# Two transformer blocks on one core: VectorE's small work around the convolution moved, and ScalarE's two norm visits put earlier

## The reference, cut to what matters

```python
proj = jnp.einsum('bld,dp->blp', n, w_in)
conv_in, gates, scal = jnp.split(proj, [CONV_CH, CONV_CH + GATE_CH], axis=-1)
c = jax.nn.silu(centred_dwconv(conv_in, conv_w, conv_b)).astype(F32)
q, k, v, xs, Bm, Cm = jnp.split(c, [...], axis=-1)
...
q = l2_normalize(q.reshape(Bsz, L, gh, GDN_HEAD_DIM)) * (GDN_HEAD_DIM ** -0.5)
k = l2_normalize(k.reshape(Bsz, L, gh, GDN_HEAD_DIM))
g_fw = -jnp.exp(gA[0]) * jax.nn.softplus(a_f + gB[0])
...
gc = jnp.cumsum(g, axis=-1)
decay = jnp.exp(jnp.where(incl, gc[..., :, None] - gc[..., None, :], -jnp.inf))
```

## Time and profile before

| | us |
|---|---|
| runs | 1373.17, 1374.37, 1367.18 |
| median | 1373.17 |
| the profiled execution: its time | 1375.73 |
| the profiled execution: its span | 1373.7 |
| TensorE busy | 1226.6 (89%) |
| VectorE busy | 645.5 (47%) |
| ScalarE busy | 410.6 (30%) |
| GpSimd busy | 331.0 (24%) |

### The profile page before, as it was taken

One profiled execution on the slowest core, in us unless ns is written; L12 is line 12 of the kernel. 1 busy time (PEld: TensorE's weight loads), 2 busy tenths in 40 slices (PEclk: granted clock), 3 DMA queues, 4 the chain that ended last, 5 costly groups with the idle time before them and its releaser, 6 DMA issues.

```text
span 1373.7 us, 17987 instructions
## 1 busy us (share of the span) xinstructions
PE 1226.6 (89%) x7446; PEld 926.1 (67%) x7446; DVE 645.5 (47%) x1059; ACT 410.6 (30%) x991; POOL 331.0 (24%) x322
## 2 busy tenths in 40 slices
PE   6989789899999699978789998998988999899887
PEld 5878655577754332212129797998878889798777
DVE  1597758133560300001026355575887245466785
ACT  4345542133631410100014521311524441230332
POOL 0386640412200300000021122132253112223231
PEclk9999989999999799999999999999999999999999
DMA  5333333766406699999982435153332245335310
GB/s 196 123 123 123 123 92 134 267 242 218 152 30 275 257 386 421 422 421 422 421 340 71 160 107 204 62 173 134 123 111 85 96 172 170 114 114 184 123 62 31
DMA packets 91554, 257.02 MB, mean 187 GB/s; under 512 B 7645, under 2 KB 12534, under 8 KB 79058
## 3 DMA queue, kind: packets, MB, share of 16 engines
q1 hardware_dynamic: 89122, 248.67, 48.3%
q0 software_dynamic: 2032, 6.95, 1.6%
q10 hardware_dynamic: 320, 0.26, 0.1%
HBM read 253.49 MB, written 2.12 MB: 186 GB/s over the span
## 4 chain that ended last, share of the span: by engine, by line
PE 63%; DMA 14%; DVE 9%; ACT 7%; POOL 5%; issue 2%; SPq 0%; DVEq 0%; ACTq 0%; POOLq 0%
PE bank L686 59%; DMA ring<-in_w_up_dram 8%; DMA ring<-in_w_down_dram 4%; PE bank L695 3%; DVE ring_r L1993 3%; POOL late L2595 3%; POOL acc L2596 2%; DVE acc L2064 2%; ACT ring L1508 1%; DMA ring<-in_w_ada_dram 1%; ACT cT L1508 1%; ACT L1508 1%; ACT oa L1508 1%; ACT qkT L1508 1%; ACT xT L1508 0%
## 5 line engine op out<-in xcount | busy, mean ns | idle before, releaser
L2698 POOL CAST w_hi_r<-ring 128x1024 fp32r<-128x1024 f32 x136 | 151.0, 1138 | 670.4 <-DMA ring<-in_w_in_dram 267.3
L686 PE MATMUL bank<-ring_r,xT_hi 128*128 128x256 f32 (+1 forms) x864 | 245.9, 285 | 0.0
L686 PE MATMUL bank<-w_hi_r,xT_hi 128*128 128x256 f32 x704 | 208.6, 296 | 24.2 <-DVE ring_r L1993 19.8
L686 PE MATMUL bank<-w_hi_r,xT_r 128*128 128x256 f32 x704 | 202.6, 288 | 0.0
L1993 DVE TENSOR_TENSOR ring_r<-ring,w_hi_r 128x1024 fp32r<-128x1024 f32 x136 | 182.6, 1375 | 41.9 <-POOL w_hi_r L2698 41.9
L686 PEld LDWEIGHTS bank<-ring_r,xT_hi 128*128 128x128 f32 x864 | 168.3, 195 | 0.2
L686 PEld LDWEIGHTS bank<-w_hi_r,xT_hi 128*128 128x128 f32 x704 | 137.2, 195 | 36.5 <-DVE ring_r L1993 25.7
L686 PEld LDWEIGHTS bank<-w_hi_r,xT_r 128*128 128x128 f32 x704 | 136.9, 195 | 0.0
L686 PE MATMUL bank<-ring,xsT 128*32 128x512 f32 x496 | 111.8, 595 | 26.4 <-DMA ring<-in_w_up_dram 13.2
L686 PE MATMUL bank<-xT,ring 128*128 128x256 f32 x576 | 127.5, 384 | 0.0
L686 PEld LDWEIGHTS bank<-xT,ring 128*128 128x128 f32 x576 | 111.0, 193 | 15.3
(11 more groups left out here) (360 smaller groups left out, 2133.0 us busy)
## 6 DMA issues: line engine op xcount, KB each, us to landing
ring<-in_w_in_dram SPq DMA_DIRECT2D x39, 2048.0 KB, 7.8
ring<-in_w_up_dram SPq DMA_DIRECT2D x32, 1024.0 KB, 16.3
ring<-in_w_down_dram SPq DMA_DIRECT2D x32, 1024.0 KB, 16.3
ring<-in_w_gate_dram SPq DMA_DIRECT2D x30, 1024.0 KB, 16.4
ring<-in_w_ada_dram SPq DMA_DIRECT2D x12, 2048.0 KB, 8.8
ring<-in_w_out_dram SPq DMA_DIRECT2D x8, 2048.0 KB, 7.7
ring<-in_w_o_mla_dram SPq DMA_DIRECT2D x2, 2048.0 KB, 12.6
ring<-in_w_o_swa_dram SPq DMA_DIRECT2D x2, 2048.0 KB, 7.8
```

Source lines behind the costliest of these rows:

```text
L686: return release(nc.tensor.matmul(o, lhsT, rhs, start=start, stop=stop))
L2698: nc.gpsimd.tensor_copy(hi, raw_).then_inc(hi_done.sem, hi_done.one("piece"))
```

## The change

VectorE begins its tile 0 as soon as the decay rates `g` are made. The copy of the running sums, `ed` and the halves come ahead of its tile 5 (`decay_sums`). The factors and the constant tiles come ahead of its tile 20 (`decay_factors`). The multiplications by the norms stand ahead of tiles 20 and 24; they stood behind tiles 24 and 32. ScalarE makes `lnd`, `eg` and `ed` inside its first norm visit. Its squares come two tiles sooner, and its second norm visit is at n = 22, where it was at n = 26. TensorE's second group of norm sums stands between pairs 10 and 11; it was between pairs 11 and 12.

```diff
-        front_dve = Steps(sem("front_dve"), "cols xn0 xn1 g gc done halves rows")
+        front_dve = Steps(sem("front_dve"), "cols xn0 xn1 g gc halves rows done")
...
                 w = take("w_in")
-                if n in (4, 6):
-                    for i in range(2 * n - 8, 2 * n - 4):
+                if n == 4:
+                    for i in range(4):
                         norm_pair(i)
                 conv_tiles(2 * n, w, 0)
+                if n == 5:
+                    for i in range(4, 8):
+                        norm_pair(i)
...
                 link(last)
+                if i0 == 0:
+                    act.wait_ge(front_dve.sem, front_dve.at("gc"))
+                    f(lnd[:], lnd[:], ACT.Ln).then_inc(front_act.sem, front_act.one("lnd"))
+                    f(eg[:], gc[:], ACT.Exp).then_inc(front_act.sem, front_act.one("eg"))
+                    f(ed[:], ed[:], ACT.Exp).then_inc(front_act.sem, front_act.one("ed"))
                 for i in range(i0, i0 + 4):
...
-                if n == 2:
-                    act.wait_ge(front_dve.sem, front_dve.at("gc"))
-                    f(lnd[:], lnd[:], ACT.Ln).then_inc(front_act.sem, front_act.one("lnd"))
-                    f(eg[:], gc[:], ACT.Exp).then_inc(front_act.sem, front_act.one("eg"))
-                    f(ed[:], ed[:], ACT.Exp).then_inc(front_act.sem, front_act.one("ed"))
                 if n >= 3:
                     conv_silu(n - 3)
-                if n >= 6 and n % 2 == 0 and n <= 20:
-                    squares(n // 2 - 3)
-                if n in (18, 26):
-                    inverse_norms(n // 2 - 9)
+                if n >= 4 and n % 2 == 0 and n <= 18:
+                    squares(n // 2 - 2)
+                if n in (18, 22):
+                    inverse_norms(n - 18)
...
             for n in conv_mine(False):
+                if n == 5:
+                    decay_sums()
+                if n == 20:
+                    decay_factors()
+                if n in (20, 24):
+                    for i in range(n - 20, n - 16):
+                        normed(i)
                 if n == 12:
...
                 ins.then_inc(conv_dve.sem, 1)
-                if n in (24, 32):
-                    for i in range(n // 2 - 12, n // 2 - 8):
-                        normed(i)
```

More of the change, by code:

```diff
@@ L2027, in _ @@
                 op1=ALU.mult).then_inc(front_dve.sem, front_dve.one("g"))
[L2028 to L2050, removed]
+            def decay_sums():
+                dve.wait_ge(front_pe.sem, front_pe.at("cs"))
+                cs = bank[5][:, 0:3 * TT * NSC].rearrange("p (m c n) -> p m c n", m=3, c=TT)
+                for d, lo, n in ((0, 0, GH), (1, GH, GH), (0, 2 * GH, SH), (1, 2 * GH + SH, SH)):
+                    last = nc.vector.tensor_copy(gc[:, :, lo:lo + n], cs[:, d, :, lo:lo + n])
+                link(last)
+                tt(ed[:], cs[:, 2], gc[:], ALU.subtract).then_inc(front_dve.sem, front_dve.one("gc"))
+                gh, gl = (halves_r[:, :, lo:lo + NSC] for lo in (0, NSC))
+                link(nc.vector.tensor_copy(gh, gc[:]))
+                tt(gl, gc[:], gh.bitcast(F32), ALU.subtract).then_inc(front_dve.sem, front_dve.one("halves"))
@@ new lines, in decay_factors @@
+            def decay_factors():
+                dve.wait_ge(load_tri, 16)
+                nc.vector.tensor_copy(eye_r[:, 0, :], tri[:, 0, :])
+                tt(hot_r[0:2 * NSC, :], tri[0:2 * NSC, 0, 0:NSC], tri[0:2 * NSC, 0, NSC:2 * NSC], ALU.add)
+                nc.vector.tensor_copy(nmask_r[:].rearrange("p (c d) n -> p c (d n)", c=TT),
+                                      tri[:, 4:6, :].rearrange("p d n -> p (d n)").unsqueeze(1).to_broadcast([P, TT, 2 * P])
+                                      ).then_inc(masks_in, 1)
+                dve.wait_ge(front_act.sem, front_act.at("ed"))
+                tt(lnd[:], lnd[:], gc[:, :, 2 * GH:NSC], ALU.subtract)
+                tt(bed[:], beta[:], ed[:, :, 0:2 * GH], ALU.mult)
+                tt(dted[:], dt[:, :, 0:NSC], ed[:], ALU.mult)
+                stt(out=nbias[:], in0=dt[:, :, NSC:NSB], scalar=-1.0, in1=gc[:, :, 0:2 * GH], op0=ALU.mult, op1=ALU.subtract)
+                ts(neg_eg[:], eg[:], -1.0, None, ALU.mult).then_inc(front_dve.sem, front_dve.one("done"))
```

## The result

The changed kernel took 1366.3 us (median of 12 runs, 1362.7 to 1369.99), the kernel before, run beside it, 1375.11 us (12 runs, 1367.18 to 1377.94). The ratio is 0.9937, with a 95% interval of 0.9924 to 0.9949. That is 0.63% or 8.7 us faster, between 7.0 and 10.4. The forecast was 1364.9 us, counted off the earlier median of 1373.17, and a gain of 8.3 us.

A forecast was written before the change was run, and what follows sets the result against it. The bound was taken to be a ring of GpSimd and ScalarE from tile 19, started by TensorE's pair 9. Terms 5.8 - 0.75 + 2.7 + 0.55 = 8.3 us off 1373.17 gave 1364.9 us, range 1360.6 to 1370.2.

The forecast's parts named there:

- TensorE's wait and its sums: Between pairs 7 and 8: the wait for gT_r goes and the norm sums take 3.62 us; gain 5.8 us.
- first visit, with lnd, eg, ed: ScalarE's first norm visit, ahead of GpSimd's tile 19, grows by lnd, eg and ed; loss 0.75 us.
- GpSimd's tiles 23 to 31: Tiles 23 and 31 shrink from 12.94 and 12.97 us to 11.6; gain 2.7 us.
- tail: From GpSimd's end to the SiLU of tile 35: one turn and one VectorE tile, instead of 5.93 us; gain 0.55 us.
- the ring: From tile 19 on, GpSimd and ScalarE release each other in turn; TensorE's pair 9 starts it, plain turn 1.60 us.
- TensorE's new wait: Second norm group, near 107 us, waits 1.3 us for ScalarE's first Exp; about 3 us of cover, cost nothing.
- The norms' multiplications: On VectorE, they move from beside GpSimd's tiles 23 and 31 into GpSimd's gaps; gain 2.7 us, bounds 0 to 2.7.
- VectorE's moved work: decay_factors (ten instructions, 1.8 us) between tiles 18 and 20 and decay_sums (1.4 us) fall into idle time; cost nothing.
- the rival of an absorbed shift: A transfer with a fixed end behind 182 us takes the shift; gain 0 to 2 us, near 1372; chance 0.05.
- The clock: TensorE's clock would fall to 1.2 GHz again ahead of the decay stage; the sum is the same either way.

The follow-up runs named there:

- e4: The kernel before, with VectorE copying gT_r ahead of its tile 9 instead of 12; ratio to the kernel before 1.0005.
- e5: The changed kernel, with VectorE copying gT_r ahead of its tile 16 instead of 12; ratio to the kernel before 0.9984.
- e9: The changed kernel, with the second norm visit back at n = 26 and its multiplications ahead of tile 28; ratio to the kernel before 0.991.
- e3: The changed kernel, with the multiplications by the norms back behind VectorE's tiles 24 and 32; ratio to the kernel before 0.9946.
- e7: The changed kernel, with ScalarE's norm visits at n = 19 and 23 instead of 18 and 22; ratio to the kernel before 0.9928.
- e8: As e7, with TensorE's second norm sums back between pairs 11 and 12; ratio to the kernel before 0.9894.
- e2: The kernel before, with only the moved squares, second norm visit, second norm sums and multiplications, VectorE's start unchanged; ratio to it 0.9969.
- e1: The changed kernel, with squares, norm visits, second norm sums and multiplications back in their old places; ratio to the kernel before 0.9957.
- e10: As e8, with lnd, eg and ed moved out of the first visit to n = 9; ratio to the kernel before 0.9891.

## Why the prediction was right, point by point

| step | predicted | measured in the two profiles |
|---|---|---|
| TensorE's wait and its sums | -5.8 | 9.39 to 3.29 us between pairs 7 and 8: -6.1 |
| first visit, with lnd, eg, ed | +0.75 | pair 9's end to tile 19: 10.06 to 10.59: +0.5 |
| GpSimd's tiles 23 to 31 | -2.7 | -1.34, +0.26, -1.24: -2.3 |
| tail | -0.55 | 5.93 to 4.66: -1.3 |
| sum | -8.3 | -9.2 (stage -9.1) |

No term is off by more than 0.8 us, and the errors (0.3, 0.2 and 0.7 us too little gain, 0.4 too much) mostly add up: only the 0.4 is offset by the others.

**TensorE's wait** counts only because GpSimd was early enough as well. The prediction named this as a condition (tile 15 done by 96.8; it was done at 94.65, which is 96.7 with the front's 2.0 us). e4 and e5 show that it is one: 0 us without the condition, 8.2 us with it. So two sentences of the prediction are too strong. VectorE's earlier start matters through two things, not one: `gT_r`, and GpSimd's earlier tile 15. And TensorE did not start the ring alone in the kernel before: ScalarE was through tap 0 of tile 18 at 106.55, and tile 15 came at 106.63.

**The first visit** cost what was predicted. From the SiLU of tile 15 to the start of tile 19 it is 8.81 us before (106.67 to 115.48) and 9.57 in the changed kernel (98.36 to 107.93): +0.76. From pair 9's end it is only +0.5, because before the SiLU of tile 15 still waited for GpSimd.

**TensorE's new wait** was 1.22 us (1.3 predicted), and it cost nothing: in e9 and in the change alike, ScalarE had pair 11 before GpSimd was done with tile 19 and then still waited 2.41 us for it.

**The norms' multiplications** are shown by e3: beside them a GpSimd tile takes 1.3 us more. The argument beside this price was wrong in one point. The prediction held that the trace shows long rows only beside the multiplications, and it took the 11.6 us beside plain convolution work for a tile's undisturbed length. The two engines slow each other there too. On VectorE's side, tile 35, alone, took 3.09 us; beside GpSimd a tile took 3.76. The multiplications themselves took 2.49 us with GpSimd idle and 3.21 beside it. On GpSimd's side, e5 has a tile 15 with VectorE idle beside it from 82.65 us on. These are its first and last instructions:

```profile
80.19 0.92 POOL L2605 TENSOR_SCALAR late<-raw,cols 128x256 f32<-128x256 f32 x1 [2.11 <-ACT acc L1511]
...
90.50 0.72 POOL L2606 TENSOR_TENSOR acc<-acc,late 128x256 f32<-128x256 f32 x1
```

It took 11.03 us, where a tile beside convolution updates took 11.6 to 11.9. So the rule of the Trainium skill (page "SBUF — State Buffer", section "Who interferes with whom"), that a VectorE instruction with two SBUF inputs contends with a GpSimd instruction that reads SBUF, agrees with the trace for both kinds. The convolution's updates cost a GpSimd tile 0.6 to 0.8 us, the multiplications 1.3 more. Whether that is for their longer row (512 elements against 256) or for the kind of instruction, no run shows. The contention with the convolution's updates is also why the gain was 2.3 us and not 2.7: tile 27 took 11.86 us beside unbroken convolution work, 0.26 more than before.

**VectorE's moved work.** `decay_factors` is eight instructions by the trace, not ten; two of the rows counted are the halves, which belong to `decay_sums`. It makes no difference to the sum: they ran ahead of 105.52 us, and VectorE was idle again from 108.01 to 110.70, ahead of tile 20.

**The tail** is the term that was mis-sized most: it was priced with 3.76 us for tile 35, and took 3.09, since GpSimd was done by then. VectorE's tile 34 was through 0.21 us before tile 35 could start, so it did not hold the tail up, but there was little to spare.

**The shift arrived** at the end. The decay stage took 193.81 - 182.06 = 11.75 us before and 182.80 - 170.93 = 11.87 us in the changed kernel. A gain of 0 to 2 us, which the rival of an absorbed shift had, is refuted by the timing (7.0 to 10.4 us).

**The clock** fell to the lower level (1.2 GHz) ahead of the decay stage as before. The windows of the changed kernel (stretch, length, busy time of PE, PEld, DVE, ACT and POOL, granted clock, DMA) show it:

```profile
165.00:170.00 5.00, 2.80 (x12) 2.71 (x13) 4.50 (x10) 2.32 (x6) 1.19 (x2) 0.50 0.15 28
170.00:175.00 5.00, 5.00 (x32) 4.86 (x32) 2.03 (x4) 4.04 (x12) 0.00 (x0) 0.71 1.03 389
175.00:185.00 10.00, 10.00 (x71) 8.55 (x70) 9.55 (x17) 9.21 (x29) 1.73 (x3) 1.00 0.04 10
```

## What to carry to other kernels

Find the ring: two engines that release each other in turn, and write down each turn's length and gap. Work that stands between "I have your result" and "here is your next input" costs its full length; the same work one step later, behind the release, ran beside the other engine. Then look at who holds the next turn: in e7 it was TensorE, and the step gave 2.3 us; with TensorE's sums moved as well (e8) it gave 6.9. Where a wait looks removable, look for a second lateness that ends at the same time: taking away one of two gives nothing (e4 and e5), and both together give all.

## What the runs showed of the hardware that was not expected

**The same front at different speeds.** TensorE's 32 matmuls on the scalars took 7.09 us in the kernel before and in seven of the experiments, 4.84 in the changed kernel, 5.24 in e7 and 3.79 in e5 and e9, with no edit ahead of them. Windows of e5 and of the changed kernel, 16.5 to 21 and 21 to 24 us:

```profile
16.50:21.00 4.50, 4.05 (x33) 3.91 (x34) 0.36 (x2) 1.69 (x4) 0.00 (x0) 1.00 1.05 407
21.00:24.00 3.00, 3.00 (x15) 2.64 (x15) 0.00 (x0) 2.93 (x5) 0.00 (x0) 1.00 1.04 385
```
```profile
16.50:21.00 4.50, 4.19 (x30) 4.19 (x31) 0.00 (x0) 1.75 (x3) 0.00 (x0) 0.81 1.05 406
21.00:24.00 3.00, 3.00 (x10) 2.55 (x10) 0.35 (x2) 1.86 (x3) 0.00 (x0) 0.50 1.04 386
```

In the second pair the clock is at its lower level (1.2 GHz) for part of the time. In the kernel before it is recorded as 1.00, and yet only 21 matmuls fit where e5 had 33; why is open:

```profile
16.50:21.00 4.50, 4.41 (x21) 4.41 (x21) 0.00 (x0) 1.53 (x3) 0.00 (x0) 1.00 1.04 402
```
Pair 3 starts anywhere between 42.20 and 47.67 us in the twelve profiles, 5.5 us of scatter, two thirds of what this change is worth.

**A second fall of the clock in the decay stage.** From the SiLU of tile 35 to the first gate matmul it took 11.75 to 11.90 us in the kernel before, the change, e2, e4, e5 and e9, but 13.14 to 13.31 us in e1, e3, e7, e8 and e10. Windows of e1:

```profile
172.00:177.00 5.00, 5.00 (x31) 4.82 (x30) 4.14 (x9) 1.60 (x6) 0.00 (x0) 0.71 0.74 240
177.00:182.00 5.00, 3.09 (x23) 2.79 (x22) 2.67 (x5) 4.99 (x17) 0.00 (x0) 0.97 0.50 185
182.00:187.00 5.00, 5.00 (x30) 4.81 (x29) 3.96 (x7) 3.04 (x12) 0.00 (x0) 0.69 0.00 0
```

In e1 TensorE was through its first four heads in 7.3 us (7.9 in the kernel before) and then waited 1.91 us (1.34 before), and the clock fell again in the heads behind. About 1.4 us of what these versions gain is lost here. This was seen, not tested by a run of its own; why the clock fell in these versions and not in the others is open.
